# Half of the expert output sums stay in PSUM over 18 groups, and gathered rows are spread differently: one Trainium2 core

## What is computed

```python
def block(args):
    xc, ic, gc = args                      # 128 tokens, their 128 experts each, their weights
    h = jnp.einsum('td,ted->te', xc, jnp.take(u, ic, axis=0))
    a = jax.nn.gelu(h, approximate=False) * gc
    return jnp.einsum('te,ted->td', a, jnp.take(v, ic, axis=0))
```

## Time and profile before

| what | value |
|---|---|
| time, median of 3 runs | 3084.58 us (3083.65 to 3088.66) |
| profiled execution, its own time | 3081.31 us |
| its span (first to last instruction) | 3079.6 us |
| mean granted TensorE clock | 0.983 of full speed |
| function experts | from about 1590 us to the end |
| first y group that the change treats (group 13) | from 2475.2 us |
| row jobs of u, of v | 1623 to 2219 us, 2219 to 3044 us |
| DMA traffic of the whole kernel | 601 MB |

### The profile page before, as it was taken

The page is one execution under the profiler, slowest core; times in us unless marked ns, Lnnn a source line. Parts: engine busy times, 40 slices in busy tenths (PEclk is TensorE's granted clock), DMA queues, the critical chain, the costliest instruction groups (busy, mean ns, idle before and its releaser), DMA issues. The chain is left out here.

```text
span 3079.6 us, 46779 instructions
## 1 busy us (share of the span) xinstructions
PE 2968.7 (96%) x17450; PEld 1663.7 (54%) x17450; DVE 2313.1 (75%) x4663; ACT 977.5 (32%) x1417; POOL 1257.6 (41%) x883
## 2 busy tenths in 40 slices
PE   7989998989999799999999999999999999999999
PEld 4445465455555577777765555555555544444444
DVE  3255376358888666666649999989999999999996
ACT  4332365134433344444432222222222222222221
POOL 1013121014243311211226666676666666566562
PEclk9999899999999899999999999999999999999999
DMA  3110100121211245545568989989999888888884
GB/s 101 55 55 15 55 1 28 62 74 63 83 56 61 93 166 198 189 176 199 188 227 290 310 302 329 316 303 315 307 308 322 290 312 296 303 298 299 300 299 168
DMA packets 258490, 601.37 MB, mean 195 GB/s; under 512 B 21025, under 2 KB 127665, under 8 KB 255281
## 3 DMA queue, kind: packets, MB, share of 16 engines
q1 hardware_dynamic: 181168, 321.78, 31.0%
q0 software_dynamic: 73728, 268.47, 24.3%
q10 hardware_dynamic: 3456, 9.44, 0.8%
HBM read 516.78 MB, written 82.84 MB: 195 GB/s over the span
## 5 line engine op out<-in xcount | busy, mean ns | idle before, releaser
L238 PE MATMUL f_y<-f_v_hi,f_a_hi 128*128 128x512 f16 x1536 | 582.4, 379 | 8.7 <-DVE p_h L2323 8.7
L239 PE MATMUL f_y<-f_v_lo,f_a_hi 128*128 128x512 f16 x1536 | 582.1, 379 | 0.0
L240 PE MATMUL f_y<-f_v_hi,f_a_lo 128*128 128x512 f16 x1536 | 582.1, 379 | 0.0
L2292 POOL DMA_INDIRECT x_rows<-in_peer_v,p_row_index x256 | 305.9, 1195 | 281.6 <-DVE p_h L2342 256.2
L2292 POOL DMA_INDIRECT x_rows<-in_peer_u,p_row_index x251 | 321.7, 1282 | 186.4 <-DVE x_rows L2332 141.9
L2332 DVE SCALAR_TENSOR_TENSOR x_rows<-x_rows,p_xs 128x1024 f32<-128x1024 f32 x256 | 378.4, 1507 | 24.7 <-DMA x_rows<-in_peer_u,p_row_index 24.5
L2342 DVE SCALAR_TENSOR_TENSOR p_h<-x_rows,f_row_a,p_h 128x1024 f32<-128x1024 f32 x256 | 384.5, 1502 | 16.6 <-DMA x_rows<-in_peer_v,p_row_index 11.4
L2301 POOL TENSOR_TENSOR f_v_lo<-f_v_in,f_v_hi 128x1024 f16<-128x1024 f32 x128 | 286.8, 2241 | 87.4 <-ACT f_v_hi L2240 85.4
L2323 DVE SCALAR_TENSOR_TENSOR p_h<-f_y,p_h 128x512 f32<-128x512 f32 x384 | 262.4, 683 | 75.9 <-PE f_y L240 75.4
L238 PE MATMUL f_hid<-p_act_hi,x_u_hi 128*128 128x384 f16 x880 | 286.9, 326 | 2.1 <-DVEq L2308 2.1
L240 PE MATMUL f_hid<-p_act_hi,x_u_lo 128*128 128x384 f16 x880 | 286.9, 326 | 0.0
(11 more groups left out here) (314 smaller groups left out, 5489.5 us busy)
## 6 DMA issues: line engine op xcount, KB each, us to landing
f_v_in<-in_peer_v SPq DMA_DIRECT2D x128, 512.0 KB, 5.6
dense_weights<-e_stage SPq DMA_DIRECT2D x24, 2048.0 KB, 7.6
f_g_in<-dense_weights SPq DMA_DIRECT2D x32, 1536.0 KB, 16.2
x_u_in<-in_peer_u SPq DMA_DIRECT2D x56, 512.0 KB, 6.2
x_gel<-early_tiles SPq DMA_DIRECT2D x72, 384.0 KB, 3.5
e_u_in<-in_peer_u SPq DMA_DIRECT2D x48, 512.0 KB, 4.1
early_tiles<-e_gel SPq DMA_DIRECT2D x48, 384.0 KB, 2.3
a_w_in<-in_w_in SPq DMA_DIRECT2D x24, 512.0 KB, 3.7
```

The costliest lines, as they stand in the source:

```text
L238: pe.matmul(out, a_hi, b_hi, start=first, stop=False)
L239: pe.matmul(out, a_hi, b_lo, start=False, stop=False)
L240: return pe.matmul(out, a_lo, b_hi, start=False, stop=last)
L2292: nc.gpsimd.indirect_dma_start(out=rows[q % ROWS][:], out_offset=None, in_=table, in_offset=bass.IndirectOffsetOnAxis(ap=T.row_index[:, ti ...
```

## The change

Three edits, all in function experts.

1. PSUM banks. From group RESIDENT = 13 on, whose outputs run when the last late tile's hidden values are done, outputs of odd k no longer alternate through y: each has a bank of its own (the two of u_ps and the four of hid), keeps summing there over all groups 13 to 31 (start only in the first, stop only in the last), and is added to h once, after the last group. Outputs of even k use the two y banks in turn, so a bank comes back after four outputs in place of two, and TensorE waits before an even k for the add of k-4. The first held output waits for the GELU and the low part of tile 55, which used these banks last.
2. VectorE skips the adds of odd k in groups 13 to 30; the counts on semaphore y_added follow (function added).
3. Row jobs: 5 for two early tiles in place of 4, that is 2 and 3 in turn, 180 in the 72 early tiles where 144 were. The 36 come from the late tiles, 332 in 52 tiles in place of 368.

TensorE's program has one more turn of eight tiles written out (the first early one) and its loop one turn less.

```diff
--- before.py
+++ after.py
@@ -2066,7 +2066,8 @@
         rows, row_hid = T.first.rows, T.row_hid
         row_a = S.sb("row_a", [P, NS, PICKS])
         u_ps = S.ps("u_ps", [P, KT, P])
-        hid = [S.ps(f"hid{b}", [P, 2, HALF])[:, :, 0:DHALF] for b in range(2)]
+        hid_banks = [S.ps(f"hid{b}", [P, 2, HALF]) for b in range(2)]
+        hid = [banks[:, :, 0:DHALF] for banks in hid_banks]
         y = [S.ps(f"y{b}", [P, HALF]) for b in range(2)]
 
         v_loaded = [S.sem(f"v_loaded{b}") for b in range(2)]
@@ -2097,15 +2098,30 @@
         y_place = [(k // 2, k % 2) for k in range(YB)]
 
 
+        RESIDENT = LATE * LOOP // GROUP - 1
+        LAST = NE // GROUP - 1
+        resident = [u_ps[:].rearrange("p k c -> p (k c)")[:, h * HALF:(h + 1) * HALF] for h in range(2)] + [
+            hid_banks[b][:, h, :] for b in range(2) for h in range(2)]
+
+        def y_bank(k, stay):
+            if not stay:
+                return y[k % 2][:]
+            return resident[k // 2] if k % 2 else y[k // 2 % 2][:]
+
+        def added(group_n, k):
+
+            return YB * RESIDENT + YB // 2 * (group_n - RESIDENT) + (k + 1) // 2
+
+
 
         UROWS = NS * PICKS
         JOBS = 2 * UROWS
         EARLY_FROM = LATE * LOOP
-        LATE_JOBS = JOBS - SPREAD_JOBS - 2 * N_EARLY
+        LATE_JOBS = JOBS - SPREAD_JOBS - 5 * N_EARLY // 2
 
         def jobs_before(n):
             late, early = min(n, EARLY_FROM), max(n - EARLY_FROM, 0)
-            return min(JOBS, SPREAD_JOBS + LATE_JOBS * max(late - GROUP, 0) // (EARLY_FROM - GROUP) + 2 * early)
+            return min(JOBS, SPREAD_JOBS + LATE_JOBS * max(late - GROUP, 0) // (EARLY_FROM - GROUP) + 5 * early // 2)
 
         def place(q):
             return q % UROWS // PICKS, q % PICKS
@@ -2156,7 +2172,7 @@
                 if t < NS:
                     sp.wait_ge(row_used, UROWS - SPREAD_JOBS + PICKS * (t + 1))
                 else:
-                    sp.wait_ge(y_added, BASE + YB * (NE // GROUP - 1) + 2 * (t - NS) + 2)
+                    sp.wait_ge(y_added, BASE + added(LAST, 0) + 2 * (t - NS) + 2)
                 sp.dma_start(out_v[:, t, :], T.h[:, t, :]).then_inc(stored, 16)
             sp.wait_ge(stored, 16 * NT)
 
@@ -2185,28 +2201,38 @@
                                         T.act_hi[:, k, toks], T.act_lo[:, k, toks], k == 0, k == KT - 1)
                 last.then_inc(hid_done, 1)
 
-            def outputs(group_n, g, part):
+            def outputs(group_n, g, part, stay=False, start=True, stop=False):
 
                 if part == 0:
                     pe.wait_ge(a_lo_done, BASE + GROUP * (group_n + 1))
                     pe.wait_ge(v_lo_done, BASE + GROUP * (group_n + 1))
                 for k in range(part * YS, (part + 1) * YS):
                     t, half = y_place[k]
-                    pe.wait_ge(y_added, BASE + YB * group_n + k - 1)
+                    held = stay and k % 2 == 1
+                    if not stay:
+                        pe.wait_ge(y_added, BASE + YB * group_n + k - 1)
+                    elif stop and k >= 4:
+                        pe.wait_ge(y_added, BASE + added(LAST, 0) + k - 3)
+                    elif not held:
+                        pe.wait_ge(y_added, BASE + added(group_n, k) - 1)
+                    elif start and k == 1:
+                        pe.wait_ge(gelu_done, BASE + EARLY_FROM)
+                        pe.wait_ge(u_lo_done, BASE + EARLY_FROM)
                     for j in range(GROUP):
                         toks, cols = slice(t * P, (t + 1) * P), slice(half * HALF, (half + 1) * HALF)
-                        last = split_mm(pe, y[k % 2][:], a_hi[g][j][:, toks], a_lo[g][j][:, toks],
-                                        v_hi[g][j][:, cols], v_lo[g][j][:, cols], j == 0, j == GROUP - 1)
+                        last = split_mm(pe, y_bank(k, stay), a_hi[g][j][:, toks], a_lo[g][j][:, toks],
+                                        v_hi[g][j][:, cols], v_lo[g][j][:, cols], j == 0 and (start or not held),
+                                        j == GROUP - 1 and (stop or not held))
                     last.then_inc(y_done, 1)
 
-            def step(c, m, y_too=True, u_too=True, early=False):
+            def step(c, m, y_too=True, u_too=True, early=False, first=False):
                 n = c * LOOP + m
                 if u_too and not early:
                     turn(n + 1, m + 1)
                 if not early:
                     hidden(n, m)
                 if y_too:
-                    outputs(2 * c + m // GROUP - 1, (m // GROUP + 1) % 2, m % GROUP)
+                    outputs(2 * c + m // GROUP - 1, (m // GROUP + 1) % 2, m % GROUP, stay=early, start=first or not early)
 
             hidden(1, 1, between=2)
             for m in range(2, LOOP):
@@ -2216,11 +2242,13 @@
                     step(c, m)
             for m in range(LOOP):
                 step(LATE - 1, m, u_too=m < LOOP - 1)
-            with pe.Fori(LATE, TURNS) as c:
+            for m in range(LOOP):
+                step(LATE, m, early=True, first=m < GROUP)
+            with pe.Fori(LATE + 1, TURNS) as c:
                 for m in range(LOOP):
                     step(c, m, early=True)
             for part in range(GROUP):
-                outputs(NE // GROUP - 1, 1, part)
+                outputs(LAST, 1, part, stay=True, start=False, stop=True)
 
         @block.scalar
         def _(act):
@@ -2318,9 +2346,15 @@
             def add_y(group_n, k):
                 t, half = y_place[k]
                 cols = slice(half * HALF, (half + 1) * HALF)
+                stay = group_n >= RESIDENT
+                if stay and k % 2 and group_n < LAST:
+                    return
                 dve.wait_ge(y_done, BASE + YB * group_n + k + 1)
-                dve.wait_ge(y_added, BASE + YB * (group_n - 1) + k + 1)
-                nc.vector.scalar_tensor_tensor(T.h[:, NS + t, cols], y[k % 2][:], 1.0 / S_A, T.h[:, NS + t, cols],
+                if group_n <= RESIDENT or k % 2:
+                    dve.wait_ge(y_added, BASE + YB * (min(group_n, RESIDENT) - 1) + k + 1)
+                else:
+                    dve.wait_ge(y_added, BASE + added(group_n - 1, k) + 1)
+                nc.vector.scalar_tensor_tensor(T.h[:, NS + t, cols], y_bank(k, stay), 1.0 / S_A, T.h[:, NS + t, cols],
                                                ALU.mult, ALU.add).then_inc(y_added, 1)
 
             def row_job(q):
```

## The result

The kernel after takes 3118.36 us (median of 4 runs, 3114.74 to 3129.29) where the kernel before takes 3085.43 (4 runs, 3083.65 to 3088.66): ratio 1.0109 [1.0085, 1.0134], slower by 1.1% or 33 us. The forecast was 3075.4 with 3091 as the upper end.

A forecast was written before the change was run, and what follows sets the result against it. TensorE was taken as the bound, with 12.4 us of waits to win. Groups 14 to 30 -5.5, group 13 -1.7 and late tiles -2.0 give -9.2: 3075.4 us from the median 3084.6, range 3070.5 to 3091.

The forecast's parts named there:

- the wait at k=3: Early groups: TensorE waits for an add queued behind a_lo, itself behind POOL's v_lo; removing it saves 0.37 us x 17.
- The adds: VectorE's adds of y outputs to h: 276 for 384, 0.60 us each, 3.6 us less per group.
- Group 13: First group with held banks: 31.2 us in place of 32.9, a gain of 1.7 us.
- the walk of one group: VectorE and POOL traced job by job through one changed early group; the loop closes at about 30.9 us.
- The late tiles: Less VectorE work there removes waits of TensorE: 2.0 us won, bounds 0 and 3.1.
- Loop (b): Early groups' loop of VectorE with POOL, whose v_lo stops VectorE: about 30.9 us per group.
- term (c): Early groups' loop of loads, from a_lo of j=1 through g_in to the next v_in: 30.65 us + d, giving 31.0.
- d: Lengthening by added gathers of the 18.1 us from g_in's issue to the next v_in's landing: taken as 0.35 us.
- Rival C: Early groups slower: g_in and v_in land later by a whole gather or more; 3096.3 us at d = 1.8, chance 0.15.
- the gaps in the loads: Early groups' load queue: gaps after each v_in, held against the case that later loads slow the kernel; no size.
- Rival B: Early groups: the wait only moves to k=0, for a_lo, at 31.45 us per group; 3079.9 us, chance 0.31.
- D: Early groups: k=4 still waits for k=0's add; time near Rival B's, chance 0.07 together with late-tile shifts.

The follow-up runs named there:

- e5: The kernel after with early tiles' gathers fetching 512 columns instead of 1024, at wrong rows (part of the sum is wrong); ratio to before 0.9943.
- e1: The kernel after with the held banks kept but row jobs put back to 8 a group; 3080.63 us, ratio to before 0.9990.
- e12: The kernel after with nine row jobs a group instead of ten, the ninth in j = 1 (2, 3, 2, 2); ratio to before 1.0115.
- e9: The kernel after with nine row jobs a group instead of ten, the ninth in j = 3 (2, 2, 2, 3); ratio to before 0.9973.
- e8: The kernel after with VectorE's early row jobs summing only 64 of 1024 columns, gathers kept whole; ratio to before 1.0100.
- e6: The kernel before with one more 512 KB load per early group on SP's queue right behind g_in; ratio to before 1.0084.
- e13: The kernel after with its ten row jobs a group placed as 2, 2, 2, 4; 3075.29 us, ratio to before 0.9968.
- e7: The kernel after with 8 row jobs a group and the early groups' g_in issued from ACT's queue; ratio to before 0.9973.

## Why the prediction was wrong, and where it was right

**Right.** The bound of before, and the wait at k=3 with its chain: it is gone in all early groups. The adds: 276 in all (page, section 5: 270 of one form, 6 of the two others), 685 ns in the mean, never stretched.

```profile
L2357 DVE SCALAR_TENSOR_TENSOR p_h<-f_y,p_h 128x512 f32<-128x512 f32 x270 | 184.8, 685 | 57.2 <-PE f_y L240 56.5
```

Group 13 (-1.85 for -1.7), and the walk of one group: in group 13, whose v_in was still early, a_lo of j = 1 ends at S+14.3 (walk: 14.1 to 14.3), the last a_lo at S+30.25 (29.8), and the group takes 31.07. The late tiles came out at -1.9 for -2.0, but one pair of executions can't show that: groups 1 to 12 take 782.9 to 785.2 us in the kernels with before's spread of the jobs and g_in on SP's queue there, and 779.7 to 784.6 in those with more jobs in the early tiles. That 18 groups can go on summing in a bank costs TensorE nothing: e5's groups are 31.08. Loop (b), 30.9, isn't seen as a bound: e5 keeps all its instructions and stands at TensorE's floor.

**Wrong: term (c).** The loop was the right one and so was its shape; its numbers were 10.9 + 1.65 + 18.1 + d = 30.65 + d with d = 0.35. Measured:
- V to a_lo of j = 1: 10.7 (10.9 in the sum, so 0.2 better). From there to g_in: 1.4 (1.65 in the sum, read from one group; it is 1.2 and 1.56 in turn).
- g_in to V with the banks alone: 19.45 in e1 where the sum had 18.1.
- The same in after: 22.3. So d, all that the change adds to those 18.1 (18.2 in the mean), is 4.1 us, 1.2 with the banks and 2.85 with the row jobs; in e12 it is 4.7.

The failed step is the sizing of d, the lengthening of g_in's stretch by added gathers, and both of its factors were wrong. The count: the walk gave one more gather ("7 for 6"); by bytes 4.6 gathers passed there in before and 7.3 do in after, so 2.7 more. The price: I took 0.35 for one, "near the landings because they measure this very transfer", between 0.15 and a whole gather's 1.5. It is the whole 1.5, since the DMA engines are busy throughout that stretch (share 1.00), and 2.7 x 1.5 = 4.1. The upper bound of d was one gather at the right price.

The landings that I preferred compare late tiles with early ones, where u_in and gel differ as well as the gathers, and a change of g_in's landing is not the change of the stretch to V.

Place against count is shown by e12 and e9, nine jobs each: 3.3 us per group apart in the profiled executions, 2.6 by the ratios of the medians (1.42% of 3085 us over 17 groups). Of the 3.3, 1.9 us are g_in's own landing (18.4 for 16.5), in which 6.44 MB pass in place of 5.60. The rest comes with gel and v_in behind it. SP issues them later as well, since the third row job stands in front of j = 2 on VectorE and gel waits for that tile's a_lo: in the mean gel of j = 0 goes out 7.4 us behind g_in in e12 and 6.3 in e9, v_in 11.2 and 9.35. So 1.8 of the 3.3 us have passed when v_in is issued, and from v_in's issue to V it is 1.5 us more.

**Rival C** was the mechanism, at a chance of 0.15, and its signs came: L2268 later than S+3.4 (S+8.2), g_in at 17 us or more (18.5). Its point of decision, 0.43, was right in kind; its d of 1.8, "a whole gather or more", was still less than half of the 4.1. And one argument that the prediction held against it, the gaps in the loads, doesn't bear: there are none between g_in's issue and V. Rival B's sign, TensorE waiting for a_lo at each group's start, is also there, as it must be whenever loop (b) or (c) binds; e8 says that it was (c). D is out: no wait for an add is left in groups 14 to 31.

The Trainium skill's rule named in the prediction (DMA: Bandwidth & Descriptors, Queues, rings and completion order), that each engine takes turns between its queues packet by packet, speaks for the whole 1.5 us of an added gather. That was nearer than the rows that I preferred, and six of the nine changed kernels in the table of bytes agree with it within 0.2 us, e6 within 0.4; e12 takes 1.1 us more, and e5, whose stretch isn't full, 1.5 more.

**The DMA share misled.** I argued for C from the mean share of 0.86 and against it from gaps. After has the same share, 0.86, and is slower; e13 has 0.92 and is faster than before. The mean share says neither yes nor no. The share of the stretch that the loop waits for does: 1.00 in the kernel before.

**Open.** Why e12's stretch holds 1.1 us more than its bytes, at a share of 0.77 behind g_in's landing. It is also argued, not shown, that VectorE's running ahead is what brings the fifth gather into e1's stretch. The runs of one kernel scatter (3059 to 3082 us in e9), more than their medians differ, so the order of e7, e9 and e13 among each other isn't settled.

## What to carry to other kernels

When a step that issues a DMA is moved, ask first where its transfer will lie against the large load that a closed loop waits for, and read the share of the DMA engines in the stretch from that load's issue to the landing that is waited for: at 1.00 every added byte costs its time there, whatever the mean over the period is (0.86 here). Count what will pass in it, in bytes, and count again for each part of the change. Write out every loop that closes over a period (here loads, VectorE and TensorE lay within half a microsecond), with the pieces of each measured in the trace; when one part of a change frees an engine, what that engine issues moves too, so its own loop has to be walked again before the second part is added. In an experiment vary the place at a fixed count as well as the count: nine jobs were worse than ten.

## What the runs showed of the hardware

In groups 15, 17, 19, 21, 28 and 30 of after 7 to 13 matmuls at or near the start are 0.42 us apart in place of 0.216, and the granted clock there is 0.50, TensorE's lower clock level (1.2 for 2.4 GHz). Ahead of these groups TensorE had been idle for 2.2 to 4.0 us, waiting for a_lo; ahead of group 23, after 3.1 us, the pace stays at 0.216. Group 17's first three, and a window from there (granted clock third from the end):

```profile
2611.55 0.60 PE L238 MATMUL f_y<-f_v_hi,f_a_hi 128*128 128x512 f16 x1 [3.54 <-DVE f_a_lo L2408]
2611.95 0.63 PE L239 MATMUL f_y<-f_v_lo,f_a_hi 128*128 128x512 f16 x1
2612.37 0.63 PE L240 MATMUL f_y<-f_v_hi,f_a_lo 128*128 128x512 f16 x1
...
2611.55:2616.55 5.00, 5.00 (x12) 1.74 (x13) 2.93 (x3) 0.00 (x0) 3.46 (x3) 0.50 1.04 394
```

It costs nothing here, since the next group waits for a_lo anyhow; where TensorE is the bound it would be 1.4 to 2.7 us a time (an estimate: 7 to 13 matmuls at 0.2 us more each). The early window's granted clock is 0.98, where it was 1.00.

SP's queue can be held up at an issue: gel of j = 0, the first DMA behind g_in, takes 3.1 us of it in the mean of after and 3.4 in before, where an issue is 0.33 to 0.38 us in most other places. In e5, with half the gathers' bytes, it takes 0.5 us, and in e8, where most gather bytes pass there, 8.2.
